# The second half of a layer joined to the first in one block, with the router's products taken from the unnormalized state

## The reference

```python
        x = x + g1 * (merged @ w_out[l])                      # output projection

        h = rmsnorm(x, norm_ffn_g[l]) * (1.0 + sc2) + sh2     # norm, scale, shift
        h2 = h.reshape(b * s, d)
        y = swiglu(h2, w_shared_gu[l], w_shared_down[l]) + moe_routed(
            h2, router_w[l], router_bias[l], w_exp_gu[l], w_exp_down[l])

    # in moe_routed
    scores = jax.nn.sigmoid((h2 @ router_w).astype(jnp.float32))
    _, idx = lax.top_k(scores + router_bias.astype(jnp.float32), TOP_K)
```

## Time and profile before

| | before |
|---|---|
| median of 3 runs | 2967.61 us |
| runs | 2962.85 to 2975.04 us |
| time of the profiled execution | 2973.13 us |
| span of the profiled execution | 2971.5 us |
| mean granted TensorE clock | 0.974 of full |
| PE busy | 2795.8 us, 94% |
| DVE busy | 2090.5 us, 70% |
| ACT busy | 1655.1 us, 56% |
| POOL busy | 671.9 us, 23% |

### The profile page before, as it was taken

How to read it: one execution, slowest core, us unless ns; L and a number is a source line. 1 busy time by engine, 2 the same in 40 slices (tenths; PEclk the granted TensorE clock), 3 DMA queues, 4 the chain that set the end, 5 groups by cost and what they waited for, 6 DMA issues and landing times. The chain is left out here.

```text
span 2971.5 us, 43967 instructions
## 1 busy us (share of the span) xinstructions
PE 2795.8 (94%) x14448; PEld 2252.5 (76%) x14448; DVE 2090.5 (70%) x2971; ACT 1655.1 (56%) x2620; POOL 671.9 (23%) x567
## 2 busy tenths in 40 slices
PE   6999999999899999999789999999989999999995
PEld 4677777777678888888566777777866888888884
DVE  5544456555688999999845444666547999999997
ACT  2442434433467888888534334344234788888883
POOL 1000000100155743333210000000001557433430
PEclk9999999999899999999889999999999999999997
DMA  7224343333489999999722343423426999999995
GB/s 249 88 71 156 117 135 102 105 121 121 190 306 361 373 360 375 363 375 361 288 69 91 106 138 110 135 87 119 139 96 234 357 363 346 374 377 366 361 347 230
DMA packets 125101, 673.17 MB, mean 227 GB/s; under 512 B 27757, under 2 KB 29165, under 8 KB 90989
## 3 DMA queue, kind: packets, MB, share of 16 engines
q1 hardware_dynamic: 91328, 606.70, 55.5%
q0 software_dynamic: 31680, 58.36, 6.0%
q10 hardware_dynamic: 1932, 6.16, 0.9%
HBM read 657.39 MB, written 55.28 MB: 240 GB/s over the span
## 5 line engine op out<-in xcount | busy, mean ns | idle before, releaser
L2205 DVE TENSOR_TENSOR ew_lo<-ew,e_hi 128x2048 fp32r<-128x2048 f32 x258 | 591.4, 2292 | 95.2 <-ACT e_hi L2001 95.2
L738 PE MATMUL bank<-h_hi,w_hi 128*128 128x512 f32 x1248 | 509.1, 408 | 27.1 <-DVE h_lo L989 8.4
L2001 ACT ACTIVATE e_hi<-ew 128x2048 fp32r<-128x2048 f32 x260 | 498.5, 1918 | 13.8 <-PE bank L2420 7.7
L738 PE MATMUL bank<-h_hi,w_lo 128*128 128x512 f32 x1248 | 501.9, 402 | 0.0
L738 PE MATMUL bank<-h_lo,w_hi 128*128 128x512 f32 x1248 | 499.6, 400 | 0.0
L673 DVE TENSOR_TENSOR w_lo<-raw,w_hi 128x1024 fp32r<-128x1024 f32 (+2 forms) x202 | 241.5, 1198 | 292.9 <-ACT w_hi L663 292.2
L2420 PE MATMUL bank<-e_hi,x_hi 128*128 128x512 f32 x1040 | 417.6, 402 | 0.1
L2420 PE MATMUL bank<-ew_lo,x_hi 128*128 128x512 f32 x1040 | 407.8, 392 | 0.0
L2420 PE MATMUL bank<-e_hi,x_lo 128*128 128x512 f32 x1040 | 405.5, 390 | 0.0
L1889 POOL DMA_INDIRECT y_d<-y,idx x130 | 214.6, 1651 | 476.2 <-issue 395.6
L738 PEld LDWEIGHTS bank<-h_hi,w_hi 128*128 128x128 f32 x1248 | 239.1, 192 | 104.0 <-issue 29.3
(11 more groups left out here) (340 smaller groups left out, 4883.6 us busy)
## 6 DMA issues: line engine op xcount, KB each, us to landing
ew<-in_wexp SPq DMA_DIRECT2D x130, 2048.0 KB, 9.8
raw<-in_wmix SPq DMA_DIRECT2D x297, 512.0 KB, 3.5
ew<-in_wexp SPq DMA_DIRECT2D x130, 1024.0 KB, 10.4
ew<-y_d SPq DMA_DIRECT2D x8, 2048.0 KB, 12.2
ew<-y_d SPq DMA_DIRECT2D x8, 1024.0 KB, 8.3
ada0a<-in_ada SPq DMA_DIRECT2D x2, 2048.0 KB, 13.4
ada0b<-in_ada SPq DMA_DIRECT2D x2, 2048.0 KB, 22.1
h_d<-htok ACTq DMA_DIRECT2D x8, 512.0 KB, 11.5
```

Of the source, the lines that this page charges most:

```text
L738: ins = nc.tensor.matmul(out, lhs, rhs, start=start, stop=stop)
L2001: nc.scalar.activation(e_hi[h][:], up_part(ew, j, h), ACT.Copy).then_inc(whi_done, 1)
L2205: nc.vector.tensor_tensor(up_part(ew_lo, j, h), up_part(ew, j, h), e_hi[h][:].bitcast(F32), ALU.subtract).then_inc(wlo_done, 1)
```

## The change

The two blocks of a layer become one. The functions `sp_experts`, `pool_experts`, `act_experts`, `dve_experts` and `pe_experts` hold what the second block held and are called at the end of each engine's stream in the first. Nothing is computed otherwise but this:

- During "out" ACT also makes `xa[k] = xT[k]*amul[k]` (`scaled_out`), and PE makes the router's products from `xa` into OB, chunk m-1 after job m. `xa` lies where the third expert's weights `ew2` come to lie. SP loads the three tables `rw`, `rcst`, `pay` in "out", behind the load of the sixth of its eight tiles.
- The sum of squares is made in two groups of one-column products: from `pr` without the last chunk, then from the last chunk's squares.
- PE makes 8 products of the shift with `rw` (64 columns) into SB[1]. Scores are `SB[0]*rstd + SB[1]` on DVE, and the sigmoid is taken of them after the turn.
- `hf = xa*MB` on DVE; ACT makes `h_hi` from it with the shift, and later adds the shift into `hf`; DVE makes `h_lo` with the shift added. PE takes jobs 0 and 1 of "shared" chunk by chunk as `h_lo` comes, and only then `rows(0)` to `rows(3)`.
- DVE has `weights_low(1)` before the top 8, `job_out(1)` after them, and `product_low(0)` and `weights_low(2)` before the wait for the ranks. POOL's two `filed` both wait for the gates.
- SP issues the fourth and fifth shared tile, then waits for `rstd`, then loads the weights of experts 0 and 1; the sixth shared tile and the weights of expert 2 come after.

The diff without its changes of indentation, and cut:

```diff
+        xa = place("xa", [P, KD, S], at=t_end["ew2"] - 24576)
 # SyncE, in the first block's loop over tiles
+                        if u == MIX_TILES - 3:
+                            sp.wait_ge(mlo_ready, KD)
+                            sp.dma_start(rw[:], rw_d[l]).then_inc(rw_in, 16)
+                            sp.dma_start(rcst[:], rcst_d).then_inc(rw_in, 16)
+                            sp.dma_start(pay[:], pay_d).then_inc(rw_in, 16)
+                    sp_experts(sp)
 # sp_experts
+                load_tile(sp, l, MIX_TILES + RAW)
+                load_tile(sp, l, MIX_TILES + RAW + 1)
+                sp.wait_ge(rstd_ready, norm_no["x2"] + 1)
                     load_up(0, 0)
                     load_down(0, 0)
                     load_up(1, 1)
                     load_down(1, 1)
-                    load_tile(sp, l, MIX_TILES + RAW)
+                for u in range(MIX_TILES + RAW + 2, NTILES):
+                    load_tile(sp, l, u)
+                sp.wait_ge(nt_ready, norm_k0["x2"] + KD)
                     load_up(2, 2)
                     load_down(2, 2)
-                    for u in range(MIX_TILES + RAW + 1, NTILES):
-                        load_tile(sp, l, u)
 # pool_experts
-                    pool.wait_ge(oh_ready, 1)
+                pool.wait_ge(gates_ready, 1)
                     pool.wait_ge(h2_out[0], 32)
 # ScalarE, "out"
+                    def scaled_out(act, k):
+                        nc.scalar.activation(xa[:, k, :], xT[:, k, :], ACT.Copy, scale=amul[:, k:k + 1]).then_inc(xa_ready, 1)
                         if m:
                             square_out(act, m - 1)
+                            scaled_out(act, m - 1)
+                    nc.scalar.activation(stat[:, 4:5], zero[:, 0:1], ACT.Sigmoid)
+                    split_hi(act, MIX_TILES)
+                    square_out(act, KD - 1)
+                    scaled_out(act, KD - 1)
+                    split_hi(act, MIX_TILES + 1)
+                    act_experts(act)
 # act_experts
+                act.wait_ge(logits_ready, 1)
+                nc.scalar.activation(sgt[0:NE, :], OB[0:NE, :], ACT.Copy).then_inc(score_ready, 1)
+                act.wait_ge(lin_ready, 1)
+                nc.scalar.activation(score[:], score[:], ACT.Sigmoid).then_inc(score_ready, 1)
+                for k in range(KD):
+                    act.wait_ge(nt_ready, norm_k0["x2"] + k + 1)
+                    nc.scalar.activation(h_hi[:, k, :], hf[:, k, :], ACT.Identity, bias=mod[:, 24 + k:25 + k]
+                                         ).then_inc(nhi_ready, 1)
+                    if k >= 2:
+                        shifted(k - 2)
+                shifted(KD - 2)
+                shifted(KD - 1)
+                act_stream(act, shared[1:3], NTILES)
+                for t in range(TC):
+                    rows(t)
+                act_stream(act, shared[3:], NTILES)
 # VectorE, dve_experts
                     split_lo(dve, MIX_TILES + 1)
+                dve.wait_ge(logits_ready, 2)
+                link(dve, nc.vector.tensor_copy(posn[:, 0, :], SB[1][:, 0:NE]))
+                dve.wait_ge(rstd_ready, norm_no["x2"] + 1)
+                for t in range(TC):
+                    ins = nc.vector.scalar_tensor_tensor(score[:, t, :], SB[0][:, t * NE:(t + 1) * NE], rstd[:, t:t + 1],
+                                                         posn[:, 0, :], ALU.mult, ALU.add)
+                wait_mb_full(dve, ("rb", "x2"))
+                for k in range(KD + 1):
+                    if k < KD:
+                        nc.vector.tensor_tensor(hf[:, k, :], xa[:, k, :], MB[:], ALU.mult).then_inc(nt_ready, 1)
+                    if k:
+                        dve.wait_ge(nhi_ready, norm_k0["x2"] + k)
+                        nc.vector.scalar_tensor_tensor(h_lo[:, k - 1, :], hf[:, k - 1, :], mod[:, 23 + k:24 + k],
+                                                       h_hi[:, k - 1, :].bitcast(F32), ALU.add, ALU.subtract
+                                                       ).then_inc(nlo_ready, 1)
+                weights_low(1)
+                dve.wait_ge(score_ready, 2)
 # TensorE, end of "out"
+                        if m == 1:
+                            pe.wait_ge(rw_in, 48)
+                        if m:
+                            logits(m - 1)
...
+                    pe.wait_ge(xs_used, KD - 2)
+                    for t in range(TC):
+                        nc.tensor.matmul(MB[:, t:t + 1], pr[2][:, t * P:(t + 1) * P], ones[:, 0:1], start=t == 0, stop=False,
+                                         skip_group_check=True)
+                    pe.wait_ge(xs_ready, KD)
...
+                    logits(KD - 1).then_inc(logits_ready, 1)
+                    for k in range(KD):
+                        nc.tensor.matmul(SB[1][:, 0:NE], mod[:, 24 + k:25 + k].broadcast_to([P, P]), rw[:, k, :],
+                                         start=k == 0, stop=k == KD - 1)
+                    pe_experts(pe)
 # pe_experts
+                for k in range(KD):
+                    shared_part(0, k, k + 1)
+                    shared_part(1, k, k + 1)
+                pe.wait_ge(hf_ready, KD)
                     for t in range(TC):
+                    rows(t)
                     shared_part(2, 0, 4)
                     pe.wait_ge(sel_ready, 1)
```

More of the change, by code:

```diff
@@ L2082, in _ @@
-                    split_lo(dve, MIX_TILES)
-                    split_lo(dve, MIX_TILES + 1)
-                    def low(k0, k1):
-                        for k in range(k0, k1):
-                            dve.wait_ge(nhi_ready, norm_k0["x2"] + k + 1)
-                            nc.vector.tensor_tensor(h_lo[:, k, :], hf[:, k, :], h_hi[:, k, :].bitcast(F32),
-                                                    ALU.subtract).then_inc(nlo_ready, 1)
-                    shared = [events_of(whole([j])) for j in jobs["shared"]]
@@ L2093, in weights_low @@
-                    def weights_low(i):
-                        dve_stream(dve, [ev for ev in shared[i] if ev[0] == "tile"], NTILES)
-                    def job_out(i):
-                        dve_stream(dve, [ev for ev in shared[i] if ev[0] == "chunk"], NTILES)
-                    def product_low(i):
-                        dve.wait_ge(shi_ready, i + 1)
-                        nc.vector.tensor_tensor(s_lo[:, i, :], sgt[:], s_hi[:, i, :].bitcast(F32),
-                                                ALU.subtract).then_inc(slo_ready, 1)
+                    chain[0] = 0
@@ new lines, in add_square @@
+                    def add_square(k):
+                        dve.wait_ge(xs_ready, k + 1)
+                        if k >= 2:
+                            dve.wait_ge(xs_used, k - 1)
+                        nc.vector.tensor_tensor(pr[2][:], pr[2][:], sn[k % 2][:], ALU.add).then_inc(xs_used, 1)
+                    for m, j in enumerate(jobs["out"]):
+                        dve_stream(dve, events_of(whole([j])))
+                        if m >= 2:
+                            add_square(m - 1)
@@ L2115, in _ @@
-                    for t in range(TC):
-                        link(dve, nc.vector.max(top[:, t, :], biased[:, t, :]))
-                        ins = nc.vector.max_index(topi[:, t, :], top[:, t, :], biased[:, t, :])
-                    link(dve, ins)
-                    low(4, KD)
-                    assert all_jobs_first[MIX_TILES] == (jobs["shared"][0].c, 0) and split_at[MIX_TILES] == MIX_TILES + 1
-                    link(dve, nc.vector.tensor_copy(topf[:], topi[:]))
-                    pairs = [P, TC, TOPK, TOPK]
@@ L2314, in _ @@
[L2314 removed]
+                    nc.vector.tensor_copy(yrow[:], pay[:, :, 0])
+                    dve.wait_ge(xr_ready, 1)
+                    nc.vector.tensor_scalar(stat[:, 0:TC], MB[:, 0:TC], 1.0 / D, EPS, ALU.mult, ALU.add).then_inc(ms_ready, 1)
+                    dve_experts(dve)
                 @block.tensor
                 def _(pe):
[L2318 to L2322 removed]
```

1690 lines of the change are left out of this document (829 added, 861 removed).

## The result

The changed kernel takes 2987.89 us, the median of 5 runs (2984.01 to 2989.94); the kernel before took 2971.78 in 5 runs (2962.85 to 2975.04). The ratio is 1.0059, with a 95% interval of 1.0046 to 1.0072. It is slower by more than the 0.5% of the text above, and lies 1.9 us above the top of the range.

What follows compares the result with a forecast made beforehand. PE bounds the expert loop; between "out" and the experts other engines' chains do. Per layer +6.8 ("out" ends later) -3.3 (job 3 sooner after it) = +3.5 us, +7.0 in two: 2974.6 us against the median 2967.61; range 2955 to 2986.

Steps and rivals of the forecast that it cites:

- the 0.5% of the text above: Whole kernel: 14.8 us, or 7.4 a layer, taken as about what a measurement can tell from no change.
- T0: End of the last "out" job in a layer, where DVE takes its result; 750.0 us in the kernel before.
- How much later T0 comes: "Out" stage: six router's products 5.2 us plus a wait for the tables 1.6 make its end 6.8 us later.
- they cost their full length: Six router's products moved into "out", where PE has no idle time: 0.86 us each, 5.2 in all.
- The wait for the tables: First router's product, behind job 1 of "out", waits 1.6 us for tables landing at 719.0; bounds 0 and 1.6 plus 2.0.
- The fall: Clock drops to half speed after the sums of squares, slowing what follows for a while; another fall in job 0 adds 2.0.
- the clock's fall at job 3 was there before too: Listed under what costs nothing: the clock's fall while PE waits for job 3 is in both kernels.
- From the gates to job 3: Gates T0+38.05, second write 1.0 later, POOL 39.05 to 45.4, DVE's s_lo and weights_low(2) 1.8 more: job 3 at T0+47.2.
- Rival three (late writes): Token writes set the time; each us the second lands later delays job 3 by one; slower by over 0.5% from 14.2; chance 0.11.
- DVE's order gives the barrier's gain back: Between jobs 0 and 3, top 8 stands behind weights_low(1) on DVE, though its scores are there at T0+10.
- The clock holds: Rival: clock stays up and tables land in time; job 3 at T0+44.8, -0.5 us a layer, 2966.6 us; chance 0.25.
- PE becomes the bound: Rival: routing chain stops being last, job 3 at T0+38.2, -5.5 us a layer, or -8.5 with clock and tables right; chance 0.08.

Runs made afterwards that it cites:

- e1: Changed kernel with the router's products of chunks 0 to 6 in one row behind the last "out" job, not one behind each job: 2976.22 us.
- e2: Changed kernel with SP issuing the three tables one tile sooner, behind the fifth tile of "out": 2981.26 us.
- e3: Changed kernel with the shift's eight products moved into "out", behind the router's product that follows job 4: 2988.15 us.
- e5: Changed kernel with products that nobody uses put into PE's waits: 2977.17 us, 1.0026 of the kernel before.
- e11: Changed kernel with the third expert's weights loaded only when all four h_d writes have landed: 2980.81 us.
- e7: Changed kernel with job 3's tile split before s_hi on ACT and weights_low(2) before s_lo on DVE: 2981.35 us.
- e4: Changed kernel with bias and top 8 ahead of weights_low(1) on DVE: 2989.72 us, 1.0064 of the kernel before.
- e10: Kernel before the change, with six unused products in PE's two waits around the spread of the root: 2966.94 us, ratio 0.9996.

## Why the prediction was wrong

The direction of the sum was right (T0 later by more than job 3 comes sooner), its size was half of what came: +3.5 us a layer was forecast, +7.3 and +7.9 were measured. Layer 0, all but the first three lines counted from T0:

| step | predicted | measured |
|---|---|---|
| router's product in "out" | 0.86 | 1.24 |
| wait for the tables | 1.6 | 1.91 |
| T0 later | 6.8 | 9.4 |
| end of the shift's products | 7.8 | 8.7 |
| first product of job 0 | 12.0 | 13.7 |
| end of job 0 | 24.2 | 25.8 |
| `sel` | 36.5 | 37.5 |
| gates | 38.05 | 39.2 |
| POOL starts | 39.05 | 41.3 |
| POOL ends | 45.4 | 47.5 |
| job 3 | 47.2 | 49.4 (50.1 in layer 1) |
| list's product sooner than before | 3.3 | 2.1 (1.5) |
| sum for a layer | +3.5 | +7.3 (+7.9) |

**The step that failed is "How much later T0 comes": "they cost their full length", put at 0.86.** The length was read from products in one row, and in "out" each stands alone between products of another kind. The job with its product is 6.69-5.44 = 1.25. Six times 0.38 are 2.3 us of the 3.8 (layer 1: 4.4) that a layer came out too low. Of the rest 0.3 is the wait for the tables, and 1.2 (1.8) lies behind T0. e1 shows the price of both kinds of place: the same products in a row cost 0.89 each, and the jobs are back at 5.44. That it is the change of kind that costs 0.38 was argued; what was shown is that it goes when the products stand together.

**The wait for the tables** was right in its mechanism and within 0.3 us; e2 takes it away.

**The clock.** The fall was foreseen, and its price in job 0 was right: from the first product to the end of job 0 it took 12.1 us, where 12.2 was put. But I had the clock back up for the spread, and it stayed down from the first small products into job 0. The shift's products took 3.68 where I chose 2.5 between bounds of 1.95 and 3.9, and the spread stayed at 2.07. These are 2.2 us, of which 1.7 are left at the first product of job 0 and 1.2 at the gates. That the small products cost more than their full-clock length because of the clock and not in themselves is shown by e3 (2.00), e1's second layer (2.00) and e5. Nowhere did the prediction count a further stretch, in which the ranks and the second half of job 2 ran at half clock (797 to 807): I wrote that the ranks "are done before they are needed", and that held, but job 2 behind them ended at 808.0, 1.1 us ahead of job 3. The text said that the clock's fall at job 3 was there before too; it moved, from PE's wait ahead of job 3 to the ranks, and the list's product came 12.8 us behind job 3 instead of 13.8. That gave 1 us back.

**From the gates to job 3.** The chain was right: writes, POOL, DVE held by the port, job 3. The wait for the second write was 2.1 us in layer 0 and 2.8 in layer 1, where I took 1.0 between 0 and 2.0: the writes took 11.8 us, no less than before, though fewer reads were in flight. e11 shows that these reads are the price all the same. The prediction had `s_hi` near T0+42, covered by POOL. It came 4 us later, at T0+45.8 and 46.3, but still inside POOL's second, which ended at T0+47.5 and 48.2; `s_lo` ended 0.5 us behind that in both layers, so POOL did cover it. ACT split job 3's tile only behind `s_hi`; e7, which takes tile and low weights ahead, shows both of them to be worth 1 to 2 us. Rival three (late writes) was at work, with 1 to 2 us a layer ahead of POOL; its own condition, writes of 14.2 us or more, was not met by the median of 11.8, and in e11, with writes of 5.0 us, the kernel is still slower than before (1.0034).

**The claim that DVE's order gives the barrier's gain back** fell with e4, for all but 0.8 us. What else gave it back is that rows, which `onehot` waits for, come behind jobs 0 and 1, and these behind the small products.

**Rivals.** "The clock holds" has its rows in layer 0 of e2 (D 103.1). "PE becomes the bound" is e5 turned round: with the clock up PE waits 6.2 us for others. So PE was near the bound only because it was slow.

What stays open: why a change between kinds of product costs 0.38 us; when in a given execution the clock falls; and why the stretch between the two layers, which no edit touches, took up to 8 us less in some profiled executions than in others.

## What to carry to other kernels

A short operation moved between long ones of another kind must be priced where it will stand: moved six times into a dense stream, it cost 1.24 us where in a row it cost 0.86 to 0.89. Put in one row, and so with two waits less in each layer, it took 11.7 us off the total. Small products between short waits should be priced at both clocks, and the time at half clock is to be added up over the whole stretch from the granted clock's rows, before and after. And before a wait is shortened or an operation moved up, it should be asked who arrives last there: filling waits took the clock of the stretch to 0.95 in both kernels, and gained some 10 us in the changed one and nothing in the one before.

## What was not expected of the hardware

- Products that nobody uses made a kernel faster: 2977.2 instead of 2987.9 us, with 16 more products a layer, and 2964.7 with them against 2968.1 without (here on two chips, and with intervals that overlap).
- The clock can fall in one layer and not in the other of the same execution, with the same instructions, and that is worth 3 to 5 us of D.
- A write of 512 KB to DRAM took 11.8 us beside the loads of one expert and a tile, and 5.0 us without the expert's.
- POOL's root took 1.85 us behind a DVE split of two inputs that had begun 0.26 us earlier, and 1.03 in the kernel before, where DVE was idle. In all traces it is 1.85 where that split runs (the changed kernel and its eleven edits, both layers) and 1.03 where it does not (the kernel before and e10). That fits a hold of POOL by DVE; no run moved the split alone:

```profile
763.53 1.85 POOL L962 TENSOR_TENSOR rstd<-stat,mhalf 128x4 f32<-128x4 f32 x1 [186.25 <-DVE stat L2465]
```

```profile
753.98 1.03 POOL L959 TENSOR_TENSOR rstd<-stat,mhalf 128x4 f32<-128x4 f32 x1 [177.02 <-DVE stat L1520]
```
